# Ten of sixteen state-space scan units moved beside the q, k, v tiles, with decays loaded by DMA

## The chip, the cores and the metric

The program runs on one core of a Trainium2 chip. The metric is the device time of one execution in microseconds, as the median of several runs. The engines of the core each take their instructions in program order: TensorE (PE) multiplies matrices into PSUM banks, VectorE (DVE) and GpSimd (POOL) do element-wise work, ScalarE (ACT) evaluates functions such as Exp, and SyncE (SP) issues the DMAs. The engines meet at semaphores alone.

## The reference, cut to what matters

The program is a hybrid layer (a state-space branch, local attention with sinks, a mixture of experts) and then two further layers. The change lies in the first layer, in the state-space branch, beside local attention:

```
dt = softplus(dt_raw + dt_bias);  a_cum = cumsum(dt * a, within a chunk of 128)
xdt = xs * dt
decay[l,s] = exp(a_cum[l] - a_cum[s]) for l >= s, else 0
cb = cm @ bm^T                          # per group and chunk
y_diag = (cb * decay) @ xdt             # per head
states = bm^T @ (xdt * exp(a_cum[end] - a_cum))
carry  = carry * exp(a_cum[end]) + states
y_off  = (cm @ carry_before) * exp(a_cum)
y = y_diag + y_off + xs * d_skip;  out = rms_norm(y * silu(z))
```

There are 512 tokens, so four chunks of 128, and 32 heads in four groups of eight. Local attention has 16 query heads on 4 key-value heads, in four blocks of 128 tokens; each block sees itself and the one before.

## The kernel before

All of it is one list of stages; every stage is a function for each engine (PE, ACT, DVE, POOL, SP), and a stage's functions are simply written behind the last stage's on each engine. Semaphores (`Stage`, with a counter per engine) carry the dependences; a `Ring` of buffers makes a taker wait for the readers of the buffer's last use. `BR` and `XR` are rings over PSUM banks 0 to 3 and 4 to 7.

Weights are fp32 and come in pieces of 1024 columns per partition, 512 KB each. `load_pieces` (SP) loads a piece, `piece_hi` (ACT) rounds it to a high half, and `piece_lo` (DVE, in the z stage every second piece on POOL) subtracts to get the low half. A product then takes three PE passes for each of eight blocks of the depth (`dense`, L442 to L444; 24 matmuls of 512 columns).

The stages around the change:

- **dt** makes the step sizes, the running sums (`NAC` holds their negative, `EAC`, `DTE`, `CDC` their exponentials) and `DA`, the steps times a.
- **qkv** has 14 steps t: two k tiles, eight q tiles (each a dense product, squares, a block sum, a root by Ln and Exp, a norm product on DVE, a rotation on PE, a sine product and a sum on DVE, a cosine product on POOL), and four v tiles of 256 columns. The steps of a tile are spread: tile t's dense product, tile t-2's rotation and tile t-1's block sum stand together in step t.
- **mix** has 20 rounds. `MIX` is the order, written by hand, and every engine follows the same list. Round r holds `s0` of scan unit r (a unit is a group g and a chunk c, four chunks of a group in a row), `s1` of unit r-1, attention's steps `a2`, `a1`, `a0` of units r-2, r-1 and r, and from round 4 on two z tiles (24 matmuls of 256 columns each, tanh on ACT, silu product on DVE, product with y on POOL). `w` splits a piece of z's weights.

In `s0`, PE makes `cb`, and for eight heads the decay exponents: a mask product (L972) and, for each head, a product of `DA` against the triangle (L976). ACT takes Exp of them with the bias `NAC` (L1085), DVE copies cb and multiplies it in (the unit's *weights*, L1127). In `s1`, PE multiplies weights and `xdt` (L988), the carried state (L998) and the new state (L1006), and DVE adds the results up: L1134 always, L1140 and L1142 where c > 0, L1149 or L1153 and L1156 where c < 3. POOL prepares xdt (L1206), its decayed copy and the skip term.

- **out** follows: gates, projections, and the rest of the layer.

Of the kernel before, what the change touches and what calls it, by code (L numbers as in the profile page):

```python
# [7 lines left out]
F32 = mybir.dt.float32  # L8
# [144 lines left out]
def const_parts():  # L153
# [15 lines left out]
    parts["negbig"] = np.where(row > col, NEG, 0.0)  # L169
# [52 lines left out]
def build(nc, d, out):  # L222
    ctx = ExitStack()
    with ctx:
# [142 lines left out]
        WR1 = ring(LOADS, w_sems[0:4])  # L367
        WRZ = ring(LOADS[0:1], w_sems[0:1])
        WRZ.prior = [WR1.of(max(n for n in range(Z_FIRST) if n % 4 == 0))]
        WR3 = ring(LOADS, w_sems[0:4])  # L370
        WR3.prior = [WRZ.of(G_FIRST - 1)] + [WR1.of(max(n for n in range(Z_FIRST) if n % 4 == i)) for i in (1, 2, 3)]
        for r in (WRZ, WR3):
            r.restart()
# [3 lines left out]
        def raw(n):  # L377
            return WR1 if n < Z_FIRST else WRZ if n < G_FIRST else WR3

# [328 lines left out]
        NAC, EAC, DTE, CDC = tiles(4, 32), tiles(4, 32), tiles(4, 32), tiles(4, 32)  # L708
        work2 = top[0]
        dx, du, dw, dl, ea = alloc(128), alloc(128), alloc(128), alloc(128), alloc(32)  # L710
        DTT = alloc(512)

# [6 lines left out]
        def dt_pe(e):  # L719
# [28 lines left out]
            m.then_inc(*D.pe.up("total"))  # L748

        def dt_dve(e):  # L750
# [29 lines left out]
            e.tensor_tensor(DTE, v3(bb.ap[:, 0:128]), NAC, ALU.add).then_inc(*bb.free(D.dve, "dte"))  # L780

        def dt_act(e):
# [8 lines left out]
            e.activation(EAC, v3(ba.ap[:, 0:128]), ACT.Exp).then_inc(*ba.free(D.act))  # L791
            e.wait_ge(*D.dve.to("dte"))
# [5 lines left out]

        top[0] = work2
        HBX, HBQ = ring(bufs(4, 512)), ring(bufs(4, 512))  # L800
# [5 lines left out]
        def qkv_ahead(t):  # L806
            n = AT["k", t] if t < 2 else AT["q", t - 2] if t < 10 else AT["v", 1]
            return min(n + 2, Z_FIRST - 1)

        def qkv_sp(e):  # L810
            load_pieces(e, AT["k", 0], Z_FIRST)
# [7 lines left out]
        def qkv_pe(e):  # L819
            for t in range(14):  # L820
                if 1 < t < 10:
                    qkv_dense(e, t)
                elif t >= 10:
# [13 lines left out]
                    if t == 13:  # L837
                        WS1.of(ns[1]).frees.update(WS1.of(ns[0]).frees)
                if 0 <= t - 4 < 2:
                    b, x = XR.take("swap", t - 4), KT[:, 2 * (t - 4), :]  # L840
# [7 lines left out]
                if 0 <= t - 2 < 10:  # L848
                    b = XR.take("rot", t - 2)
# [3 lines left out]
                    e.matmul(b.ap[:, :], C["rot"], HBX.of(t - 2).ap, start=True, stop=True).then_inc(*K.pe.up("rot", t - 2))  # L853
                if 0 <= t - 1 < 10:
                    b = XR.take("blk", t - 1)
# [5 lines left out]
        def qkv_act(e):  # L861
            for t in range(14):
                piece_hi(e, qkv_ahead(t))
                if t < 10:
                    b, x, q = BR.of("qkv", t), HBX.take(t), HBQ.take(t)
                    for s, n in x.before + q.before:
                        e.wait_ge(s, n)
                    e.wait_ge(*K.pe.to("mm", t))
                    e.activation(x.ap, b.ap[:, :], ACT.Copy).then_inc(*K.act.up("cp", t))
# [2660 lines left out]
```

## Time and profile before

| | us |
|---|---|
| median of 3 runs | 2756.09 (2755.23 to 2756.17) |
| profiled execution | 2754.79 |
| its span | 2752.8 |
| PE busy in the span | 2578.9 |
| DVE / ACT / POOL busy | 1130.6 / 1037.7 / 843.0 |

Over the whole span PE is busy for 94% of the time, and 67% of the chain of work that ended last is PE's. In a table of stretches each engine has its busy microseconds with the number of its instructions, and then the clock that TensorE was granted (1.00 is 2.4 GHz, 0.50 is 1.2 GHz). In a timeline a row has start, duration, engine, line and operation, and in square brackets how long the engine had been idle before, and what ended that.

### The profile page before, as it was taken

What the parts mean: (1) busy time and instruction counts of PE and PEld (TensorE: products, weight loads), DVE (VectorE), ACT (ScalarE), POOL (GpSimd) and SP (SyncE); (2) the same over time, 40 slices, a digit from 0 to 9 for tenths busy, and PEclk for the clock granted to TensorE, in tenths of its full rate; (3) what the DMA queues carried; (4) which work ended last, traced back from release to release, by engine and by line L of the source; (5) the groups of instructions that cost most, each with busy time, mean ns of one, the idle gap of its engine ahead of it and who ended that gap; (6) DMA issues with size and microseconds to landing.
All of it is one profiled execution on the core that took longest, in us unless ns stands there. A gap on an engine that the chain in (4) does not pass through costs nothing.

```text
span 2752.8 us, 41999 instructions
## 1 busy us (share of the span) xinstructions
PE 2578.9 (94%) x16790; PEld 2120.6 (77%) x16790; DVE 1130.6 (41%) x2008; ACT 1037.7 (38%) x2142; POOL 843.0 (31%) x538
## 2 busy tenths in 40 slices
PE   7999899999978888888999989999999999999999
PEld 6877788888865555555888879999999887778877
DVE  7854666332232111111456653224247776412212
ACT  5444454432222211213455554322334555532231
POOL 1002565312321222200311105644641110465563
PEclk9999999999989999999999999999999999999999
DMA  4230111333349999998311112323322111233331
GB/s 147 82 83 23 32 32 39 108 92 92 104 170 390 426 426 426 427 423 337 93 47 55 47 39 73 97 79 91 100 78 77 47 52 42 61 89 95 100 99 62
DMA packets 311731, 370.43 MB, mean 135 GB/s; under 512 B 10208, under 2 KB 283744, under 8 KB 286960
## 3 DMA queue, kind: packets, MB, share of 16 engines
q1 hardware_dynamic: 310384, 363.52, 37.7%
q0 software_dynamic: 1152, 4.19, 0.4%
q8 instruction: 136, 2.23, 0.3%
q14 instruction: 59, 0.48, 0.1%
HBM read 363.49 MB, written 4.19 MB: 134 GB/s over the span
## 4 chain that ended last, share of the span: by engine, by line
PE 67%; DMA 12%; DVE 9%; ACT 5%; POOL 3%; issue 3%; SPq 0%; ACTq 0%; DVEq 0%; POOLq 0%
DMA early<-in_w_up_e 11%; PE bank L2406 5%; PE bank L1900 5%; PE bank L2407 5%; PE bank L2408 5%; PE bank L2913 4%; PE bank L2914 4%; PE bank L2915 4%; PE bank L442 4%; PE bank L444 4%; PE bank L443 4%; POOL split L2381 2%; DVE early L683 2%; PE bank L1060 1%; PE bank L1062 1%
## 5 line engine op out<-in xcount | busy, mean ns | idle before, releaser
L2381 POOL TENSOR_TENSOR split<-keep,split 128x1024 fp32r<-128x1024 f32 x143 | 352.3, 2468 | 452.7 <-ACT split L2355 452.7
L2406 PE MATMUL bank<-x_hi,split 128*128 128x264 f32 (+1 forms) x1280 | 396.9, 310 | 11.3 <-POOL split L2381 9.6
L2407 PE MATMUL bank<-x_lo,split 128*128 128x264 f32 (+1 forms) x1280 | 390.1, 305 | 0.0
L2408 PE MATMUL bank<-x_hi,split 128*128 128x264 f32 (+1 forms) x1280 | 389.8, 305 | 0.0
L2355 ACT ACTIVATE split<-keep 128x1024 fp32r<-128x1024 f32 x192 | 200.2, 1050 | 222.8 <-PE bank L2915 208.1
L1900 PE MATMUL bank<-early 128*64 128x256 f32 x2048 | 238.2, 386 | 38.0 <-DMA early<-in_w_up_e 32.6
L2406 PEld LDWEIGHTS bank<-x_hi,split 128*128 128x128 f32 x1280 | 240.9, 188 | 32.4 <-issue 19.2
L1900 PEld LDWEIGHTS bank<-early 128*64 128x64 f32 x2048 | 165.9, 139 | 121.1 <-issue 73.6
L2407 PEld LDWEIGHTS bank<-x_lo,split 128*128 128x128 f32 x1280 | 241.1, 188 | 9.9 <-issue 0.2
L2408 PEld LDWEIGHTS bank<-x_hi,split 128*128 128x128 f32 x1280 | 240.1, 188 | 10.2
L2951 DVE TENSOR_TENSOR mlp<-mlp,bank 128x264 f32<-128x264 f32 (+1 forms) x96 | 49.5, 515 | 326.6 <-ACT mlp L2930 326.6
L2913 PE MATMUL bank<-hidden0h,split 128*128 128x264 f32 x512 | 145.5, 284 | 1.2 <-issue 1.2
L2914 PE MATMUL bank<-hidden0l,split 128*128 128x264 f32 x512 | 145.1, 283 | 0.0
L2915 PE MATMUL bank<-hidden0h,split 128*128 128x264 f32 x512 | 145.0, 283 | 0.0
L414 ACT ACTIVATE w_split<-early 128x1024 fp32r<-128x1024 f32 (+1 forms) x101 | 105.6, 1046 | 100.7 <-PE bank L444 97.0
L2018 DVE TENSOR_TENSOR early<-early,bank 128x256 f32<-128x256 f32 x32 | 13.5, 421 | 314.4 <-PE bank L1941 189.4
L2961 DVE TENSOR_TENSOR mlp<-bank,roots 128x264 f32<-128x264 f32 (+1 forms) x96 | 46.8, 515 | 228.9 <-PE bank L2915 228.9
L1924 PE MATMUL bank<-early 128*64 128x512 f32 x512 | 116.9, 598 | 21.4 <-DVE early L2025 21.4
L428 DVE TENSOR_TENSOR w_split<-early,w_split 128x1024 fp32r<-128x1024 f32 (+1 forms) x70 | 89.9, 1284 | 95.3 <-ACT w_split L414 95.3
L442 PE MATMUL bank<-x_hi,w_split 128*128 128x512 f32 x304 | 123.8, 407 | 1.3 <-DVE w_split L428 0.7
L2930 ACT ACTIVATE mlp<-bank 128x264 f32<-128x264 f32 (+1 forms) x96 | 43.6, 454 | 202.4 <-PE bank L2408 202.4
L444 PE MATMUL bank<-x_hi,w_split 128*128 128x512 f32 x304 | 118.8, 391 | 0.0
(490 smaller groups left out, 6127.4 us busy)
## 6 DMA issues: line engine op xcount, KB each, us to landing
early<-in_w_gate_e SPq DMA_DIRECT2D x64, 1024.0 KB, 10.9
early<-in_w_up_e SPq DMA_DIRECT2D x64, 1024.0 KB, 11.8
early<-in_w_down_e SPq DMA_DIRECT2D x64, 1024.0 KB, 11.2
early<-in_w_in SPq DMA_DIRECT2D x68, 512.0 KB, 3.7
keep<-in_mlp_w_in SPq DMA_DIRECT2D x64, 512.0 KB, 3.9
keep<-in_mlp_w_out SPq DMA_DIRECT2D x64, 512.0 KB, 4.0
keep<-in_a_w_qkv SPq DMA_DIRECT2D x24, 512.0 KB, 3.6
early<-in_w_ssd_out SPq DMA_DIRECT2D x16, 512.0 KB, 3.9
```

The source lines that it names most:

```text
L442: e.matmul(o, hi[:, k, :], xh, start=first and k == 0, stop=False, skip_group_check=True)
L444: m = e.matmul(o, lo[:, k, :], xh, start=False, stop=last and k == 7, skip_group_check=True)
L1900: m = e.matmul(b.ap[cols(j, 64), o:o + 256], x.ap[:, k, cols(j, 64)], wtile(us[j], 8, 256)[:, k, :], start=k == 0, stop=k == 7, skip_group ...
L1924: m = e.matmul(b.ap[cols(j, 64), :], ht.ap[:, f * 128 + 64 * j:f * 128 + 64 * j + 64], wtile(us[j], 2, 1024)[:, f, cols(q, 512)], start=f ...
L2355: e.activation(hi, x, ACT.Copy).then_inc(*S.act.up("hi", n))
L2381: e.tensor_tensor(lo, x, whole(hi), ALU.subtract).then_inc(*u.free(sig_, "lo", n))
L2406: e.matmul(o, hi[:, k, :], xh, start=k == 0, stop=False, skip_group_check=True)
L2407: e.matmul(o, hi[:, k, :], xl, start=False, stop=False, skip_group_check=True)
L2408: m = e.matmul(o, lo[:, k, :], xh, start=False, stop=k == 7, skip_group_check=True)
L2913: e.matmul(o, hi[:, k, :], yh[:, k, n0 - at:n1 - at], start=k == 0, stop=False, skip_group_check=True)
L2914: e.matmul(o, hi[:, k, :], yl[:, k, n0 - at:n1 - at], start=False, stop=False, skip_group_check=True)
L2915: m = e.matmul(o, lo[:, k, :], yh[:, k, n0 - at:n1 - at], start=False, stop=k == 7, skip_group_check=True)
```

## The change

1. **Decays by DMA.** The dt stage also makes the running sums with heads on partitions (four small products, `acumT`), DVE copies them to `AROWS`, SP writes them to DRAM (`decay_rows`), and for each scan unit `decay_sp` loads the eight rows of the unit, broadcast to all partitions, 128 x 1024 values. ACT takes Relu of (own sum - row) with a bias for each head, eight times 128 columns, and one Exp of the negative over 1024 columns. The upper triangle is masked on DVE, when cb is read (`cb_dve`, in the place of the copy). The mask product and the eight products per unit are gone from PE.
2. **Ten units beside the tiles.** `cb_pe`, `decay_act`, `cb_dve` and `scan_pool` of unit t-4, and `scan_pe`, `weights_dve` and `scan_dve` of unit t-5 stand in step t of qkv, from t = 4. Rotation, swap and block sums use `BR` in place of `XR`; raw weight pieces have three buffers there in place of four; q and k are worked on in their final place.
3. **Mix has 19 rounds.** Round r holds s0 of unit r+10 and s1 of unit r+9, attention's a2, a1, b0 and a0 of units r-3, r-2, r-1 and r (b0 is the end of the softmax: denominator, reciprocal, probabilities), and z tiles from the first round on, two a round in 13 rounds, then one.
4. `weights_dve` of a unit stands in the round of its products, ahead of them, and no longer in the round before. The slot of the first of z's two split pieces is freed half-way in the last tile that reads it, and the first weights of out may be loaded as soon as their buffers are free.

```diff
+        K_FIRST = AT["k", 0]
+        WRQ = ring([LOADS[i] for i in (2, 3, 0)], [w_sems[i] for i in (2, 3, 0)])
...
+            br = XR.take("acumT")
...
+                m = e.matmul(br.ap[0:32, c * 128:c * 128 + 128], DA[:, c, :], C["upto"], start=True, stop=True, skip_group_check=True)
...
+        def decay_sp(e, i):
...
+            rows = arows[8 * g:8 * g + 8, 128 * c:128 * c + 128].unsqueeze(0).to_broadcast([128, 8, 128])
+            e.dma_start(h8(x.ap), rows).then_inc(*x.landing())
...
+        def decay_act(e, i):
...
+            for j in range(8):
+                h, y = g * 8 + j, x.ap[:, cols(j, 128)]
+                e.activation(y, y, ACT.Relu, bias=AC[:, c, h:h + 1], scale=-1.0).then_inc(*M.act.up())
+            e.wait_ge(*M.act.now())
+            e.activation(x.ap, x.ap, ACT.Exp, scale=-1.0).then_inc(*M.act.up("decay", i))
...
+            e.tensor_tensor(q.ap, b.ap[:, 0:128], C["upto"], ALU.mult).then_inc(*b.free(M.dve, "cb", i))
...
         def qkv_sp(e):
-            load_pieces(e, AT["k", 0], Z_FIRST)
+            done = K_FIRST
+            for t in range(14):
...
+                if t == 2:
+                    e.wait_ge(*D.dve.to("acumT"))
+                    e.dma_start(arows, AROWS[0:32, :]).then_inc(*d_arows.land(0))
+                    e.wait_ge(*d_arows.to(0))
+                if t + 1 >= S_FIRST:
+                    decay_sp(e, t + 1 - S_FIRST)
...
+                if t >= S_FIRST:
+                    cb_pe(e, t - S_FIRST)
+                if t > S_FIRST:
+                    scan_pe(e, t - 1 - S_FIRST)
...
                 piece_lo(e, qkv_ahead(t), False)
+                if t > S_FIRST:
+                    weights_dve(e, t - 1 - S_FIRST)
...
+        Z_ROUNDS = [[2 * r, 2 * r + 1] if r < 13 else [13 + r] for r in range(19)]
         MIX = []
...
+            MIX += [(f, r + S_BESIDE - lag) for f, lag in (("s0", 0), ("s1", 1)) if r + S_BESIDE - lag < 16]
+            MIX += [(f, r - lag) for f, lag in (("a2", 3), ("a1", 2), ("b0", 1), ("a0", 0)) if 0 <= r - lag < 16]
+            MIX += [("z", j) for j in Z_ROUNDS[r]]
...
-            e.wait_ge(*M.pe.to("pv", 15))
```

What VectorE has in its row for one tile of qkv before (L888 sine product, L891 sum, L897 norm product, L428 lo half of a weight piece):

```order
L428 TENSOR_TENSOR w_split_51<-early,w_split_51 128x1024 [waits wsplit_act]
L888 TENSOR_TENSOR early<-bank5,early 128x512 [waits qkv_pe]
L891 TENSOR_TENSOR early<-early 128x512 [waits qkv_pool,qkv_dve]
L897 SCALAR_TENSOR_TENSOR early<-early,lasting 128x512 [waits qkv_act]
```

And now, for a tile beside which a unit with c = 2 is scanned (L903 the unit's weights, L1058, L1061 and L1066 the tile's three, L897 the masked cb of the next unit, L911 to L933 the unit's results, then the next tile's lo half L429 and the next unit's weights):

```order
L903 TENSOR_TENSOR early<-early 128x1024 [waits mix_act,mix_dve]
L1058 TENSOR_TENSOR early<-bank0,early 128x512 [waits qkv_pe]
L1061 TENSOR_TENSOR early<-early 128x512 [waits qkv_pool,qkv_dve]
L1066 SCALAR_TENSOR_TENSOR early<-early,lasting 128x512 [waits qkv_act]
L897 TENSOR_TENSOR early<-bank7,lasting 128x128 [waits mix_dve,mix_pe]
L911 TENSOR_TENSOR early<-early,bank4 128x512 [waits mix_pool,mix_pe]
L917 TENSOR_TENSOR ints<-bank5,early 128x512 [waits mix_pe,mix_dve]
L919 TENSOR_TENSOR early<-early,ints 128x512 [waits mix_dve]
L930 TENSOR_TENSOR early<-early 128x512 [waits mix_dve,mix_pe]
L933 TENSOR_TENSOR early<-early,bank6 128x512 [waits mix_pe,mix_dve]
L429 TENSOR_TENSOR w_split_51<-early,w_split_51 128x1024 [waits wsplit_act]
L903 TENSOR_TENSOR early<-early 128x1024 [waits mix_act,mix_dve]
```

Seven instructions have come between one tile's norm product and the next tile's sine product. On PE, the same tile after its dense product, before (L853 rotation, L859 block sum):

```order
L853 MATMUL bank5<-early,lasting 128x512 [waits qkv_dve,qkv_act]
L859 MATMUL bank6<-early,lasting 128x512 [waits qkv_act]
```

And now (L849 cb of the next unit, L861 the unit's y products, L871 carried state, L879 new state, L1019 rotation, L1025 block sum):

```order
L849 MATMUL bank7<-early 128x128 [waits mix_dve]
L861 MATMUL bank4<-early 128x64 [waits mix_pool,mix_dve]
L861 MATMUL bank4<-early 128x64 x7
L871 MATMUL bank5<-early 128x512 [waits mix_dve]
L879 MATMUL bank6<-early 128x512 [waits mix_pool,mix_dve]
L1019 MATMUL bank1<-early,lasting 128x512 [waits qkv_dve,qkv_act]
L1025 MATMUL bank2<-early,lasting 128x512 [waits qkv_act,qkv_dve]
```

Rotation and block sum now stand behind products that wait for the unit's weights. In mix, VectorE at the turn of a round before (L1188 silu products of the two z tiles, L1124 and L1127 cb and weights of the unit that PE multiplies one round later, L1134 and L1149 results of the unit before):

```order
L1188 SCALAR_TENSOR_TENSOR early<-early,bank2 128x256 [waits z_act]
L1188 SCALAR_TENSOR_TENSOR early<-early,bank3 128x256 [waits z_act]
L1124 COPY early<-bank7 128x128 [waits mix_dve,mix_pe]
L1127 TENSOR_TENSOR early<-early 128x1024 [waits mix_act,mix_dve]
L1134 TENSOR_TENSOR early<-early,bank6 128x512 [waits mix_pool,mix_pe]
L1149 COPY early<-bank7 128x512 [waits mix_pe,mix_dve]
```

And now (L1273 silu products, L903 weights of the unit that PE multiplies in this round, L897 cb, L911 to L933 its results):

```order
L1273 SCALAR_TENSOR_TENSOR early<-early,bank2 128x256 [waits z_act]
L1273 SCALAR_TENSOR_TENSOR early<-early,bank3 128x256 [waits z_act]
L903 TENSOR_TENSOR early<-early 128x1024 [waits mix_act,mix_dve]
L897 TENSOR_TENSOR early<-bank5,lasting 128x128 [waits mix_dve,mix_pe]
L911 TENSOR_TENSOR early<-early,bank6 128x512 [waits mix_pool,mix_pe]
L917 TENSOR_TENSOR ints<-bank7,early 128x512 [waits mix_pe,mix_dve]
L919 TENSOR_TENSOR early<-early,ints 128x512 [waits mix_dve]
L930 TENSOR_TENSOR early<-early 128x512 [waits mix_dve,mix_pe]
L933 TENSOR_TENSOR early<-early,bank4 128x512 [waits mix_pe,mix_dve]
```

The weights are now those of the same round's y products, and stand behind the silu products of the round before.

## Rows read from the trace of the kernel before

**Rows 1.** Table of stretches: busy us (instructions) by engine, clock, DMA share, GB/s.

```profile
205.70:265.60 59.90, 59.90 (x278) 44.34 (x277) 24.87 (x34) 25.55 (x39) 14.05 (x12) 1.00 0.09 27
265.60:312.40 46.80, 38.17 (x244) 28.53 (x244) 26.81 (x56) 22.56 (x85) 20.25 (x16) 0.89 0.08 23
...
205.70:514.20 308.50, 296.07 (x2022) 244.30 (x2022) 177.66 (x295) 139.84 (x403) 145.78 (x108) 0.98 0.14 40
```

**Rows 2.** Chain that ended last, in order of time: start us, us, what.

```profile
220.59 1.06 PE bank L853 x2
...
352.79 0.86 PE bank L1006 x2
...
377.57 0.89 PE bank L976 x8
378.69 0.89 PE bank L976 x8
379.58 1.73 PE bank L988 x16
...
384.27 1.06 PE bank L1019 x8
```

**Rows 3.** Timeline of VectorE, then of ScalarE, in a q tile and a mix round.

```profile
228.88 0.69 DVE L888 TENSOR_TENSOR early<-bank,early 128x512 f32<-128x512 f32 x1 [2.53 <-PE bank L853]
...
232.33 1.22 DVE L428 TENSOR_TENSOR w_split<-early,w_split 128x1024 fp32r<-128x1024 f32 x1
236.08 0.69 DVE L888 TENSOR_TENSOR early<-bank,early 128x512 f32<-128x512 f32 x1 [2.53 <-PE bank L853]
...
230.46 0.63 ACT L880 ACTIVATE early<-early 128x512 f32<-128x512 f32 x1
231.00 1.04 ACT L414 ACTIVATE w_split<-early 128x1024 fp32r<-128x1024 f32 x1
...
423.64 2.16 ACT L1085 ACTIVATE early<-bank,early 128x128 f32<-128x128 f32 x8
```

**Rows 4.** DMA issues of the page: out<-in, queue, count, size, us to landing.

```profile
early<-in_w_in SPq DMA_DIRECT2D x68, 512.0 KB, 3.7
```

**Rows 5.** Groups of 262 to 516 us, then two lines: ns min/median/max.

```profile
L1134 DVE TENSOR_TENSOR early<-early,bank 128x512 f32<-128x512 f32 x16 | 10.8, 674 | 0.0
L1142 DVE TENSOR_TENSOR early<-early 128x512 f32<-128x512 f32 x12 | 12.5, 1041 | 0.4
L1153 DVE TENSOR_TENSOR early<-early 128x512 f32<-128x512 f32 x8 | 8.0, 998 | 0.0
...
L1127 DVE TENSOR_TENSOR early<-early x16: 1224/1459/3357, 270.6 to 469.1; 128x1024 f32<-128x1024 f32 x16
...
L1206 POOL TENSOR_TENSOR early<-early x16: 1037/1756/2039, 263.1 to 471.3; 128x512 f32<-128x512 f32 x16
```

**Rows 6.** Timeline of ScalarE, VectorE and GpSimd at the last z tiles.

```profile
488.10 0.39 ACT L1115 ACTIVATE early<-bank 128x256 f32<-128x256 f32 x1 [2.29 <-PE bank L1062]
490.98 0.39 ACT L1115 ACTIVATE early<-bank 128x256 f32<-128x256 f32 x1 [2.49 <-PE bank L1062]
...
491.39 0.42 DVE L1188 SCALAR_TENSOR_TENSOR early<-early,bank 128x256 f32<-128x256 f32 x1 [2.46 <-ACT early L1115]
...
492.59 2.40 POOL L428 TENSOR_TENSOR w_split<-early,w_split 128x1024 fp32r<-128x1024 f32 x1
```

**Rows 7.** PE's timeline after three gaps, and stretches after the first and third.

```profile
288.20 2.07 PE L998 MATMUL bank<-early 128*128 128x512 f32 x2 [4.03 <-DVE early L1124]
...
309.59 1.13 PE L998 MATMUL bank<-early 128*128 128x512 f32 x2 [2.16 <-DVE early L1124]
...
501.18 0.35 PE L1060 MATMUL bank<-w_split,x_hi 128*128 128x256 f32 x1 [3.34 <-DVE w_split L428]
...
290.00:294.00 4.00, 4.00 (x11) 1.35 (x9) 3.11 (x5) 0.39 (x1) 1.94 (x2) 0.50 0.27 95
...
502.30:505.60 3.30, 3.30 (x18) 3.30 (x17) 0.00 (x0) 0.00 (x0) 0.00 (x0) 0.51 1.05 297
```

More of the change, by code:

```diff
@@ L707, in build @@
         top[0] = work
-        NAC, EAC, DTE, CDC = tiles(4, 32), tiles(4, 32), tiles(4, 32), tiles(4, 32)
+        NAC, EAC, DTE, CDC, AC = (tiles(4, 32) for _ in range(5))
         work2 = top[0]
@@ L796, in build @@
         program.append((dt_pe, dt_act, dt_dve, None, dt_sp))
+        M = Stage("mix")
+        ZS = Stage("z")
         top[0] = work2
-        HBX, HBQ = ring(bufs(4, 512)), ring(bufs(4, 512))
+        HBQ_ = bufs(3, 512)
+        HBQ = ring(HBQ_)
+        CBR, XD = ring(bufs(1, 128)), ring(bufs(1, 512))
+        AROWS = alloc(512)
+        XE = ring([AROWS])
+        STATE = ring(bufs(2, 512))
+        ex_sems = [sig(f"decay{i}_landed") for i in range(2)]
+        EX = ring([alloc(1024), LOADS[1]], ex_sems)
@@ new lines, in build, with h8, cols @@
+        EX.prior = [None, WR1.of(max(n for n in range(K_FIRST) if n % 4 == 1))]
+        EX.restart()
+        TMP = ring([IT[:, 0:512].bitcast(F32)])
+        assert top[0] <= NA - 16
+        SSD_UNITS = [(g, c) for g in range(4) for c in range(4)]
+        S_FIRST, S_BESIDE = 4, 10
+        def h8(a):
+            return a.rearrange("p (j n) -> p j n", j=8)
+        def cols(i, n):
+            return slice(i * n, i * n + n)
+        def decay_sp(e, i):
+            g, c = SSD_UNITS[i]
+            x = EX.take(i)
+            for s, n in x.before:
+                e.wait_ge(s, n)
+            rows = arows[8 * g:8 * g + 8, 128 * c:128 * c + 128].unsqueeze(0).to_broadcast([128, 8, 128])
+            e.dma_start(h8(x.ap), rows).then_inc(*x.landing())
@@ L923, in build @@
-        ZR = ring(bufs(2, 256))
-        MASK = halves("mask", top[0], 2, 128)
-        top[0] += 256
-        IDENTR, NEGR = MASK[:, 0, :], MASK[:, 1, :]
+            for t in range(2, 14):
+                if t < 12:
+                    x = qkv_out(t - 2)
+                    e.wait_ge(*K.dve.to("sin", t - 2))
+                    e.tensor_tensor(x, x, COS, ALU.mult).then_inc(*K.pool.up("cos", t - 2))
+                if t == S_FIRST:
+                    e.wait_ge(*X.act.to("turned", 15))
+                    e.wait_ge(*D.act.to("done"))
+                    e.wait_ge(*d_arows.to(0))
+                if t >= S_FIRST:
+                    scan_pool(e, t - S_FIRST)
@@ L1075, in mix_act @@
                 if what == "s0":
[L1076 to L1086 removed]
+                    decay_act(e, i)
                 if what == "a0":
```

335 lines of the change are left out of this document (168 added, 167 removed).

## The prediction

> **What bounds the kernel now.** I read the table of stretches first [rows 1], because the change touches only what lies between the fifth of the q, k, v tiles (205.7 us) and the last z tile (514.2 us). In these 308.5 us TensorE is busy for 296.1 us. The first stretch (tiles 4 to 13) has no gap at all; the second (four mix rounds without z tiles) has 8.6 us of gaps; and 3.3 us before 501.2 are one more [rows 7], which leaves 0.5 us of gaps for all the rounds with two z tiles. So PE bounds this part, and the change can win only what it takes off PE, plus those gaps. VectorE is busy for 177.7 us of the 308.5, ScalarE 139.8, GpSimd 145.8: no engine but PE is near its limit by its sum. What decides is therefore the order in which each engine meets its work, not the sums.
>
> **What it removes.** Each scan unit loses two mask products and eight products against the triangle on PE. The chain shows one half of a unit at 0.89 us for its eight records, and 1.12 us from one half to the next (378.69 after 377.57, with the mask product between) [rows 2]. So 16 units x 2 x 1.12 = 35.8 us leave PE. With all gaps closed as well (12.4 us) the stretch could shrink by 48.2 us at most. The four new products for the running sums (four of 128 columns, under 1 us) stand in the dt stage, ahead of the stretch; I take them at nothing, since they are ready before PE's next product has its squares, and at 1 us if not.
>
> **What it adds.** On ScalarE eight Relu of 128 columns, priced like the eight Exp they replace (2.16 us together [rows 3]), and one Exp over 1024 columns. No row has that; a copy of 1024 columns takes 1.04 [rows 3], so I take 1.05; the eight Exp of 128 before, at 2.16, bound it above. The DMA per unit is 512 KB in pieces of 512 bytes, like one weight piece: 3.7 us to landing [rows 4]. A unit's load leaves when products of the unit two before are done, about two tiles ahead of its use, so even 15 us would be hidden. On SP weight loads stand behind it, with a tile or more in hand.
>
> **What it moves: the tiles.** In the new order VectorE does in tile t: lo half of a weight piece, weights of unit t-5, sine product, sum, norm product, mask product of unit t-4, results of unit t-5. PE does in tile t: dense, products of unit t-5, rotation t-2, block sum t-1. The weights of the *next* unit thus stand behind the norm product, which waits for ScalarE's root, which waits for the block sum, which PE does after the products of *this* unit. That is a closed cycle. Count from the start S of the sine product:
> - VectorE: to the end of the norm product 3.5 us (228.88 to 232.4, where the lo half follows it [rows 3]); mask product 0.3 (128 columns); results of the unit. These are 1.35 us where c is 0 (two operations that read PSUM, 0.67 each), 4.1 where c is 1 or 2 (three that read PSUM, and two between SBUF tiles of 1.04 and 1.0), 2.4 where c is 3 [rows 5]; then lo 1.22 [rows 3] and weights 1.25 (the lower end of rows 5: GpSimd is mostly through by then).
> - ScalarE: root ready at S+2.2 (230.46 + 0.63 [rows 3]), Relu and Exp 3.3, then hi 0.95 more: the lo half can't start before S+6.45.
> - So the weights are done at S+9.0 (c 0 or 3, by ScalarE) or S+10.4 (c 1 or 2, by VectorE). Then PE: 1.75 us for eight y products, about 0.9 each for carried state and new state [rows 2], 1.05 to the sine product.
>
> The dense tile takes 7.2 - 1.9 = 5.3 us (distance of sine products without swap, less rotation and block sum [rows 3]), so PE is through with it at S+6.4 and waits. S of tile 4 is at 213.5 (205.7 + 5.3 + 0.2 + 1.0 swap + 1.05, rounded up). The next steps: 13.6 (with the second swap), 13.5, 14.9, 14.0, 12.6, 11.2 (no piece to split), 14.1; that is 307.4. Then the weights of unit 7 after 10.1, its products 2.65, and tiles 12 and 13 with unit 8 about 5.9: tiles end at **326.1** instead of 265.6, +60.5 us, with ten units masked and nine multiplied. PE idles in gaps of 2.6, 2.6, 4.0, 4.0, 2.6, 2.7, 5.6 and 7.1 us there.
>
> **What it moves: the mix.** Now a round starts on PE with the y products of a unit, whose weights VectorE makes after the *second* z product of the round before. PE ends its z tile, tanh starts 0.4 us later, the silu product ends at +1.2 (490.98, 491.39 [rows 6]), weights 1.25 more: 2.5 us of gap, less 0.2 for the mask matrix. After every second round a piece's hi and lo halves stand ahead of the weights: 2.3 us more. A z tile is 2.88 us [rows 6], attention 1.0 for each of its three PE steps [rows 2] (half for the first block row), and the exponentials end before the second z tile does, as before, so they cost nothing. From weights to weights: 14.3, 12.1, 14.0, 12.3, 16.0, 13.7 = 82.4. The first round is 2 us late, because its second z piece is loaded behind the decays of unit 10 on SP. 326.1 + 1.7 (first weights) + 2 + 82.4 = 412.2; + 11.1 to the end of that round: 423.3. Rounds 7 to 12 have no scan: 8.8 each on PE; in every other one the lo half on GpSimd (2.40 us [rows 6], behind its z product) holds the z tiles up by 1.4: 57.0. Rounds 13 to 18 with one z tile: 5.9, then 7.1 and 9.2 (scores wait for a bank behind the exponentials; in round 15 for the piece), then 4.9, 4.9, 3.9: 35.9. The end: **516.2**. The 3.3 us wait before 501.2 [rows 7] is gone within that.
>
> So order and durations alone give 516.2 against 514.2, **+2.0 us**: all that PE is rid of comes back as PE waiting for VectorE.
>
> **Two things on top.** After gaps PE's clock falls. After 4.03 us without work (288.20) a pair of records of 512 columns took 2.07 us in place of 1.06 [rows 2], and PE was still at 0.50 (1.2 of 2.4 GHz) until 294; after 2.16 us (309.59) the pair took 1.13, so the clock held; after 3.34 us (501.18) it ran at 0.51 for 3.3 us [rows 7]. Of the gaps counted above seven are over 3.2 us and seven between 2.0 and 2.7; I take half of these too. A spell of 3.3 us at half speed loses 1.6 us of PE work, and that work lies on the cycle: 10.5 x 1.6 = 17 us. The bounds are 0 and 14 x 3 (spells of 6 us, like the one from 288 to 294) = 42. Second, VectorE's operations between SBUF tiles stretch when GpSimd works: the 1024-column one from 1.22 to 3.36, and the two of 512 columns take 1.04 and 1.0 on average where those that read PSUM take 0.67 [rows 5]. These means are in the sum already; GpSimd's three products now stand beside the sum and the norm product of each tile. I add 3 us (bounds -5, all unhindered, to +15).
>
> The Trainium skill (SBUF — State Buffer, "two separate sides") says that a VectorE operation with two SBUF inputs and a GpSimd operation exclude each other for a whole instruction. The stretched rows agree. If VectorE lost every race to GpSimd's three products of 1.05 us (the lower end in rows 5), the rule would make it 3 us in each of some 13 cycles, 41 us in place of my 3; the means in the rows are well under that.
>
> **Sum.** +2 + 17 + 3 = +22 us. The profiled execution took 2754.8 (span 2752.8 and 2.0 around it), 1.3 below the median; against the median 2756.1: **2778**. Nothing after 514 us changes its order, and out's first weights are loaded earlier than they are needed in both kernels, so the shift is carried to the end.
>
> **Rivals.**
> - *Clock holds, GpSimd stays out of the way.* The cycles close as counted, yet gaps cause no half-speed spells, and the 2.04 us of work between SBUF tiles in each unit with c 1 or 2 shrinks to the 1.35 of operations that read PSUM (eight units, 5.5 us). 516.2 - 5.5 = 510.7, 3.5 below; with 0.1 us off each of the 25 or so waits that I rounded up it is 6 below: some 2750. For it: gaps of 2.0 to 2.6 are the commoner ones. Against it: both gaps over 3.2 us in the rows were followed by half speed. It decides if fewer than two spells occur. Faster: 0.12.
> - *The cycle is not there.* If weights were always ready, PE would bound as before: 2756 - 48 = 2708. Each wait above is one engine's fixed order, so this needs durations 3 us shorter per cycle. 0.02, within the faster case.
> - *A tie.* A few spells only, 2757 to 2761: 0.16.
> - *Worse.* Most gaps bring the long spell, and GpSimd's products win the port: 42 + 15 on top of 2, less what overlaps, some +48: 2804. 0.22.
> - *Forecast*, 2762 to 2792: 0.48.
>
> An edit of 0.2% (5.5 us) is about what a measurement can tell from no change. Faster 0.14, same 0.16, slower 0.70. The range 2752 to 2806 leaves out the big gain and the far tails.
>
> **What would show it.** Right: PE's first y product of each unit in tiles 5 to 12 preceded by 2.5 to 7 us of idle time released by VectorE's weights; sine products 12 to 16 us apart instead of 7.2; tiles ending near 326 to 340 us; the mix stage some 190 to 200 us long instead of 248.6; PE's clock at half speed in many of the spells after these gaps; no wait for the decay loads. Wrong: sine products 11 us apart (PE bound), y products that follow the dense tile at once, or ScalarE waiting for decays to land.

## The result, and the profile after

| | us |
|---|---|
| median before, on the same chip | 2756.13 (2755.23 to 2757.68) |
| median after | **2809.78** (2808.63 to 2812.76) |
| ratio after / before | 1.0196, 95% interval 1.0178 to 1.0213 |
| profiled execution after, its span | 2808.63, 2806.8 |

The change makes the kernel slower by 53.7 us. The forecast was slower by 22 (2778), and its range ended at 2806: the direction was right, the size was not.

The busy time of the engines in the page of the changed kernel:

```profile
PE 2585.2 (92%) x16510; PEld 2114.5 (75%) x16510; DVE 1145.8 (41%) x2009; ACT 1055.8 (38%) x2157; POOL 826.5 (29%) x538
```

PE has some 36 us less to do and is busy for 6 us *longer* than before (2585.2 against 2578.9). The table of stretches of the changed kernel says why; its columns are those of [rows 1], and the four stretches are the tiles, the passage to the mix, the rounds with scan products, and the rest up to z's end:

```profile
205.70:355.50 149.80, 118.32 (x472) 85.45 (x470) 70.10 (x87) 58.12 (x128) 43.28 (x35) 0.78 0.17 44
355.50:367.00 11.50, 0.06 (x1) 0.00 (x0) 2.88 (x3) 5.18 (x11) 4.39 (x4) 0.58 0.31 91
367.00:480.00 113.00, 95.25 (x544) 75.00 (x545) 53.86 (x107) 44.12 (x129) 43.05 (x37) 0.79 0.22 57
480.00:574.00 94.00, 90.36 (x717) 77.14 (x717) 44.74 (x102) 51.43 (x152) 42.00 (x33) 1.00 0.21 59
...
205.70:574.30 368.60, 304.29 (x1734) 237.89 (x1733) 171.58 (x296) 158.85 (x418) 132.72 (x108) 0.83 0.20 53
```

Two things are to be seen against [rows 1]. The stretch is 368.6 us long where it was 308.5, with 64.3 us of PE's idle time where there were 12.4. And the granted clock is 0.78 and 0.79 in two long stretches, 0.83 over the whole, where it was 0.98. So PE both waits and runs slowly between its waits.

PE's timeline at the y products of units 1 and 2 (tiles), 9 (the first round), 10, 14 and 15. A row's own time is that of 16 short records, the bracket is the idle time ahead of it:

```profile
240.63 3.00 PE L861 MATMUL bank<-early 128*128 128x64 f32 x16 [2.58 <-DVE early L903]
...
259.51 3.65 PE L861 MATMUL bank<-early 128*128 128x64 f32 x16 [4.37 <-DVE early L903]
...
367.25 3.65 PE L861 MATMUL bank<-early 128*128 128x64 f32 x16 [11.69 <-DVE early L903]
...
383.17 2.25 PE L861 MATMUL bank<-early 128*128 128x64 f32 x16 [1.89 <-DVE early L903]
...
449.40 3.52 PE L861 MATMUL bank<-early 128*128 128x64 f32 x16 [1.95 <-DVE early L903]
...
468.67 3.65 PE L861 MATMUL bank<-early 128*128 128x64 f32 x16 [4.06 <-DVE early L903]
```

Every one is preceded by idle time that the unit's weights (L903) end: the waits are where the forecast put them. Most are also as long as it put them: in the tiles 2.6, 4.4, 4.4 and 2.6 us ahead of units 1 to 4, where it had 2.6, 4.0, 4.0 and 2.6, and about 2 and 4 in turn in the mix. Ahead of units 5 to 7 they are 3.8 to 3.9 (forecast 2.7, 5.6 and 7.1 ahead of units 5, 6 and 7), ahead of unit 8 there is none, and ahead of unit 9 the wait is three times the forecast's. What the forecast made too small is the second column. The 16 records take 1.9 to 2.0 us at full clock (rows further down); here they take from 2.25 to 3.65, the latter being half speed throughout, and this after gaps of 1.9 us as well as after those of 4.

VectorE and ScalarE between two sine products of the changed kernel, in the cycle that the forecast described:

```profile
254.41 0.68 DVE L917 TENSOR_TENSOR ints<-bank,early 128x512 f32<-128x512 f32 x1
255.12 0.69 DVE L919 TENSOR_TENSOR early<-early,ints 128x512 f32<-128x512 f32 x1
255.73 0.68 DVE L930 TENSOR_TENSOR early<-early 128x512 f32<-128x512 f32 x1
...
258.19 1.22 DVE L903 TENSOR_TENSOR early<-early 128x1024 f32<-128x1024 f32 x1
266.92 0.69 DVE L1058 TENSOR_TENSOR early<-bank,early 128x512 f32<-128x512 f32 x1 [7.51 <-PE bank L1019]
269.09 1.45 DVE L1061 TENSOR_TENSOR early<-early 128x512 f32<-128x512 f32 x1 [1.48 <-POOL early L1082]
270.46 1.53 DVE L1066 SCALAR_TENSOR_TENSOR early<-early,lasting 128x512 f32<-128x512 f32 x1
```

The weights are ready at 259.41, and the next sine product (L1058) starts 7.5 us later. At full clock PE needs 4.6 us for what lies between (y products at 258.17, sine product at 262.73 in the kernel with six needless products, below).

### The profile page after: what moved, and what is told of

Same layout as the page of the kernel before. It is cut to its first block, busy times and chain, and to the rows that moved or that the text cites. A ratio compares the mean times of both kernels' runs of the same rounds, so it can differ in the third digit from the quotient of the medians.

```text
span 2806.8 us, 41459 instructions
## 1 busy us (share of the span) xinstructions
PE 2585.2 (92%) x16510; PEld 2114.5 (75%) x16510; DVE 1145.8 (41%) x2009; ACT 1055.8 (38%) x2157; POOL 826.5 (29%) x538
## 4 chain that ended last, share of the span: by engine, by line
PE 64%; DMA 12%; DVE 9%; issue 6%; ACT 5%; POOL 5%; SPq 0%; ACTq 0%; DVEq 0%; POOLq 0%
DMA early<-in_w_up_e 11%; PE bank L2478 5%; PE bank L2480 5%; PE bank L2479 5%; PE bank L1972 5%; PE bank L2985 4%; PE bank L2986 4%; PE bank L2987 4%; PE bank L443 3%; PE bank L444 3%; PE bank L445 3%; POOL split L2453 2%; DVE early L684 2%; PE bank L861 1%; PE bank L1186 1%
## 5 line engine op out<-in xcount | busy, mean ns | idle before, releaser
L2090 DVE TENSOR_TENSOR early<-early,bank 128x256 f32<-128x256 f32 x32 | 13.5, 421 | 314.9 <-PE bank L2013 198.1
L429 DVE TENSOR_TENSOR w_split<-early,w_split 128x1024 fp32r<-128x1024 f32 (+1 forms) x70 | 87.4, 1248 | 103.6 <-ACT w_split L415 103.6
## 6 DMA issues: line engine op xcount, KB each, us to landing
early<-in_w_gate_e SPq DMA_DIRECT2D x64, 1024.0 KB, 11.2
```

## The experiments

The theory from the trace (**the clock**): the order itself costs little, as forecast, and the rest is PE at half speed after each wait. Its rivals: the order costs more than was counted, in the tiles' cycle, in the mix rounds or at the passage between them.

### Needless products in the waits

```diff
             for s, n in b.before:
                 e.wait_ge(s, n)
+            for _ in range(3 if i < S_BESIDE - 1 else 2):
+                e.matmul(b.ap[:, :], C["ones"], R[:, 0, 16:T2], start=True, stop=True, skip_group_check=True)
             e.wait_ge(*M.dve.to("weights", i))
```

> The changed kernel, with idle gaps of TensorE filled: ahead of each wait for a unit's weights PE makes three needless products (two in the mix rounds) of 512 columns, 0.86 us each, into the bank that the y products then overwrite. Nothing else changes, and the weights come no earlier. Theory A (the half-speed clock after each gap is what I under-sized): the products after each gap run at full speed, the stretch from weights to sine product falls from about 8 to about 4.5 us in seven tiles (24 us) and the rounds with a scan lose about 3 us each (15 to 18 us): 2765 to 2780 us. Theory B (the length of VectorE's and GpSimd's chain is the cost, the clock only goes with it): within 5 us of 2810, as the chain is no shorter; if the filler delays the weights' users, slower.

Measured: 2787.55 us (2783.37 to 2790.09), ratio 1.012 (1.010 to 1.014), so 22 us less by adding work to PE. That is short of what the clock theory wanted. The trace of this kernel says why; two y products and the stretch of the tiles:

```profile
251.98 2.46 PE L863 MATMUL bank<-early 128*128 128x64 f32 x16 [1.76 <-DVE early L905]
...
284.16 2.00 PE L863 MATMUL bank<-early 128*128 128x64 f32 x16 [0.41 <-DVE early L905]
...
205.70:355.50 149.80, 129.94 (x556) 86.50 (x554) 76.58 (x94) 64.19 (x138) 49.74 (x40) 0.92 0.21 53
```

Three products (2.6 us) don't fill a wait of over 4 us. The 1.76 us that stay idle are followed by slow records (2.46), the 0.41 by full speed (2.00), and the clock comes back to 0.92 only.

### Twice as many

The same with `range(6 if i < S_BESIDE - 1 else 4)`.

> The changed kernel with six needless products of 512 columns (four in the mix rounds) ahead of each unit's y products, where three (two) gave 2787.6 us and left 2.3 us of idle time before each. Six take 3.5 us at full clock, so they should close the gaps but for the one of 11.7 us. Nothing of VectorE's or ScalarE's work is changed. Theory A (half speed follows any idle time here, and the order alone costs 2 to 10 us over the kernel before): with no gap left the granted clock is over 0.97 in 205 to 355 us and the time falls to 2760 to 2780, though the needless products themselves delay the y products where weights come early. Rival B (most of the loss is the order itself, the clock was worth just the 22 us that three products gave back): 2785 to 2800.

Measured: 2795.37 us (2791.10 to 2797.42), ratio 1.0138 (1.0121 to 1.0155): by its number a hit for the rival. But the tiles of this kernel read:

```profile
205.70:355.50 149.80, 141.06 (x588) 90.46 (x586) 71.42 (x87) 59.98 (x129) 48.13 (x38) 1.00 0.19 50
...
253.02 5.32 PE L859 MATMUL bank<-lasting 128*128 128x512 f32 x12
258.17 1.89 PE L863 MATMUL bank<-early 128*128 128x64 f32 x16
```

The clock is 1.00, as theory A wanted. Six products take 5.32 us, though, and not the 3.5 that I had expected of them. This unit's weights ended at 257.47 and its y products began at 258.17, 0.7 us late; for other units it is up to 4.2 us. Over the nine units beside the tiles these delays sum to some 18 us, each on the cycle. So this run could not tell the theories apart, and it called for one that fills the waits to their length.

### Filled to the length of each wait, and only the long ones filled

```diff
-            for _ in range(3 if i < S_BESIDE - 1 else 2):
+            for _ in range([3,3,5,5,3,2,4,4,1,13,2,4,2,4,3,4][i]):
```

and, for the second kernel, `[0,0,5,5,0,0,4,4,1,13,0,4,0,4,0,4]`.

> The changed kernel with as many needless products of 512 columns (0.86 us each) before each unit's y products as fit into its wait and no more: 3, 3, 5, 5, 3, 2, 4, 4, 1 for units 0 to 8, 13 for unit 9, then 2, 4, 2, 4, 3, 4. The waits are those of the kernel with six and four of them, from the start of the first needless product to the end of the unit's weights (2.6, 2.6, 4.5, 4.5, 3.1, 2.3, 3.7, 3.7, 1.0, 12.0, 2.0, 3.9, 2.2, 3.9, 2.7, 4.2 us), so y products start when the weights are there and PE is idle for less than 0.9 us ahead of each. Theory A (all that the needless products did in that kernel was to keep the clock, and to be late by 0.7 to 4.2 us per unit, 17.7 us in the tiles and 3.1 in the mix): that kernel's 2795.4 less 20.8 and less the 2 us of half speed after unit 9's wait, 2773; from the changed kernel's side, 2809.8 less some 42 of clock, 2768. So 2764 to 2776, the last z product at 530 to 536 us, the granted clock 0.98 or more from 205 us on. Rival B (part of the loss is in the order itself, in waits that shift as soon as PE is faster): 2780 to 2790.

> The same, but only the waits over 3.5 us are filled (units 2, 3, 6, 7, 9, 11, 13, 15; unit 8 keeps its one); the seven waits of 1.9 to 3.1 us (units 0, 1, 4, 5, 10, 12, 14) stay idle. Theory A (in this order a gap of about 2 us brings half speed by itself, and the forecast that only half of them do was wrong): each costs what the section between y products and sine product is longer in the changed kernel than in the one with six needless products, 3.4, 3.4, 1.8 and some 2.7 in the tiles and about 1.9 in each of three mix rounds, 17 us: 2780 to 2792, with the first y products of these units at 2.3 to 3.7 us for 16 records in place of 1.9. Rival B (the short gaps fell to half speed only because long ones stood around them): within 4 us of the kernel in which all are filled.

Measured: **2766.40** us (2763.33 to 2768.51), ratio 1.0043 (1.0026 to 1.0060), with all waits filled, and 2788.98 (2783.04 to 2793.26), ratio 1.0117 (1.0097 to 1.0138), with only the long ones filled. Both are what theory A wanted. The first kernel: its stretch up to z's end, the y products of unit 2, and a last z product:

```profile
205.70:533.00 327.30, 313.94 (x1870) 231.48 (x1870) 179.15 (x298) 160.39 (x422) 136.71 (x109) 1.00 0.23 63
...
252.95 2.00 PE L863 MATMUL bank<-early 128*128 128x64 f32 x16
...
530.78 0.28 PE L1190 MATMUL bank<-w_split,x_hi 128*128 128x256 f32 x1
```

The order is the same, there is some needless work more on PE, and the time is 43.4 us less (42 by the two ratios): that is the price of the clock in this change. The durations on the other engines are the same but for some of VectorE's beside GpSimd: four units' weights took 1.36 to 2.06 us there, and 1.22 in the changed kernel. What is left over the kernel before is about 12 us (2766.4 against the 2754.6 measured beside it).

In the second kernel the gaps of about 2 us are back:

```profile
240.27 3.39 PE L863 MATMUL bank<-early 128*128 128x64 f32 x16 [2.56 <-DVE early L905]
...
302.49 3.65 PE L863 MATMUL bank<-early 128*128 128x64 f32 x16 [3.52 <-DVE early L905]
...
368.07 1.97 PE L863 MATMUL bank<-early 128*128 128x64 f32 x16 [2.30 <-DVE early L905]
369.88 1.65 PE L873 MATMUL bank<-early 128*128 128x512 f32 x2
...
368.00:374.00 6.00, 5.93 (x28) 3.50 (x28) 3.31 (x5) 2.31 (x6) 4.88 (x4) 0.72 0.34 72
```

Seven gaps left open, the longest of them 3.52 us, cost 22.6 us by the medians (3.2 each) and 18 by the traces at z's end (549.1 against 531.1, 2.6 each; expected 17), with no other wait unfilled. So the gaps of 2 to 3.5 us bring half speed by themselves, not because longer ones stood around them. The last three rows show that the y products alone don't tell it: after 2.30 us their 16 records still ran at full clock, but the carried state right behind them took 1.65 us instead of 1.08, and the clock over the 6 us is 0.72. The same holds behind the open gap of 2.57 us at 224.59 (1.97 us for the 16 records, clock 0.71 from there to 230).

### Unit 9's weights in the last tile step

```diff
                 if t > S_FIRST:
                     scan_dve(e, t - 1 - S_FIRST)
+            weights_dve(e, S_BESIDE - 1)
...
-                    weights_dve(e, i - 1)
+                    if i > S_BESIDE:
+                        weights_dve(e, i - 1)
                     cb_dve(e, i)
```

> The changed kernel, but the weights of unit 9 are made at the end of the q, k, v steps on VectorE, ahead of the low half of z's second piece and no longer behind it. PE stands for 11.7 us before the y products of unit 9 (355.6 to 367.2). If that wait is the low half's, which waits for the load of z's second piece, which waits for the low half of the first on GpSimd: y products of unit 9 start near 357.5, and 6 to 10 us are saved unless the z tiles wait for the same piece behind them: 2800 to 2806. If the decays of unit 9 or their load are late instead: no change, 2810.

Measured: 2803.61 us (2801.32 to 2808.04), ratio 1.0172 (1.0152 to 1.0193): 6 us less, as expected. That is little more than the spread of the executions, but in the traces, too, the y products of unit 15 start 6.6 us earlier (462.08 against 468.67). What the edit gets around is the wait of 11.69 us ahead of 367.25. These are the rows of the changed kernel on GpSimd, SyncE, ScalarE and VectorE in that wait:

```profile
357.69 2.34 POOL L429 TENSOR_TENSOR w_split<-early,w_split 128x1024 fp32r<-128x1024 f32 x1
360.06 0.37 SPq L392 DMA_DIRECT2D early<-in_w_in  x1
363.70 1.06 ACT L415 ACTIVATE w_split<-early 128x1024 fp32r<-128x1024 f32 x1 [6.30 <-DMA early<-in_w_in]
...
364.79 1.23 DVE L429 TENSOR_TENSOR w_split<-early,w_split 128x1024 fp32r<-128x1024 f32 x1 [8.62 <-ACT w_split L415]
365.93 1.22 DVE L903 TENSOR_TENSOR early<-early 128x1024 f32<-128x1024 f32 x1
```

GpSimd splits z's *first* piece, behind its scan products; only then is the buffer free and the second piece loaded; ScalarE rounds it, VectorE splits it, and the weights stand behind that. With the weights ahead of it, unit 9's y products start at 358.19, and the wait for the second piece shows up later, in front of a z product. Rows of this kernel:

```profile
358.19 3.65 PE L861 MATMUL bank<-early 128*128 128x64 f32 x16 [2.35 <-DVE early L903]
368.34 0.55 PE L1187 MATMUL bank<-w_split,x_hi 128*128 128x256 f32 x1 [2.71 <-DVE w_split L429]
```

### The tiles' cycle opened

```diff
-                if t > S_FIRST:
-                    scan_pe(e, t - 1 - S_FIRST)
                 if 0 <= t - 4 < 2:
...
                     e.matmul(b.ap[:, :], C["blk"], HBQ.of(t - 1).ap, start=True, stop=True).then_inc(*K.pe.up("blk", t - 1))
+                if t > S_FIRST:
+                    scan_pe(e, t - 1 - S_FIRST)
```

> The changed kernel, but in the q, k, v steps PE makes a unit's products behind the rotation and the block sum of that step in place of ahead of them. Theory of the cycle (weights, products, rotation, sine, norm product, results, low half, weights): it is cut, so sine products come 11 to 13 us apart in place of 15 to 18, the tiles end 20 to 40 us earlier: 2770 to 2790. Rival (VectorE's sum of work in a tile beside GpSimd bounds): no gain over 5 us. If the clock is still half after the gaps that are left, the gain is at the lower end.

Measured: 2751.81 us (2749.92 to 2757.86), ratio 0.9987 (0.9975 to 1.0000): 58 us less than the change as made, by moving one line past two. The sine product no longer waits for the scan products, and so the next weights don't wait for the last ones. The stretch of nine steps of the tiles, and the sine product with the weights ahead of it:

```profile
199.40:282.90 83.50, 82.22 (x391) 60.24 (x390) 57.90 (x72) 52.71 (x110) 34.65 (x29) 1.00 0.29 78
...
223.00 1.22 DVE L903 TENSOR_TENSOR early<-early 128x1024 f32<-128x1024 f32 x1
224.14 0.68 DVE L1058 TENSOR_TENSOR early<-bank,early 128x512 f32<-128x512 f32 x1
...
226.88 1.53 DVE L1066 SCALAR_TENSOR_TENSOR early<-early,lasting 128x512 f32<-128x512 f32 x1
```

PE is busy for 82.2 of 83.5 us at full clock, and sine products are 7.5 to 10.9 us apart where a unit is scanned beside them (15.0 to 18.3 in the changed kernel). I had expected 2770 to 2790: I had priced the waits and not the clock that comes back with them.

### Weights one round ahead in the mix

```diff
-                    weights_dve(e, i - 1)
+                    if i == S_BESIDE:
+                        weights_dve(e, i - 1)
                     cb_dve(e, i)
...
-                    if i == 15:
-                        weights_dve(e, i)
                     scan_dve(e, i)
...
                     e.tensor_scalar(q.ap[:, 4:8], q.ap[:, 0:4], -1.0, None, ALU.mult).then_inc(*M.dve.up("max", i))
+                    if i + S_BESIDE < 16:
+                        weights_dve(e, i + S_BESIDE)
```

> The changed kernel, but in the mix rounds VectorE makes a unit's weights behind attention's maximum of the round before, ahead of the z products, as the kernel before did, and not at the start of the unit's own round. If the weights' place is what makes PE wait 1.9 to 4.1 us at the start of six rounds (with half speed behind each), these gaps vanish: 17 us of gaps and about 15 us of slow products, so 2780 to 2790. Rival (the decays on ScalarE or VectorE's sum bound the rounds): under 8 us of gain.

Measured: 2776.20 us (2774.58 to 2778.25), ratio 1.0074 (1.0054 to 1.0094): 34 us less, and again more than I had expected (2780 to 2790). The y products of a later unit and the stretch of the mix, where the clock was 0.79:

```profile
402.87 1.97 PE L861 MATMUL bank<-early 128*128 128x64 f32 x16 [0.38 <-DVE early L903]
...
367.00:480.00 113.00, 109.73 (x808) 92.57 (x808) 79.19 (x144) 62.94 (x190) 60.30 (x50) 0.96 0.26 71
```

### All three, and then z's first piece earlier

The three edits together; and with them

```diff
+                if t == 12:
+                    piece_lo(e, Z_FIRST, True)
                 if t >= S_FIRST:
                     scan_pool(e, t - S_FIRST)
...
+                if t == 13:
+                    load_pieces(e, Z_FIRST + 1, Z_FIRST + 2)
```

> Three edits of the changed kernel at once, each of which alone gave: scan products behind rotation and block sum in the q, k, v tiles (-58 us), weights of a mix round made one round ahead, behind attention's maxima (-34 us), weights of unit 9 at the end of the tiles (-6 us). Theory A (each edit cures a separate place: the tiles' cycle, the mix rounds' wait, the first round's wait, and with the gaps gone the clock stays up): they add, 2810 - 58 - 34 - 6 = 2712, range 2702 to 2722; TensorE's granted clock 0.95 or more in 367 to 480 us. Rival B (the share of the clock was counted in two of the edits at once, and TensorE's own gaps elsewhere take its place): 2730 to 2745. If TensorE had the 35.8 us of decay products taken off it and no new wait put in, before's 2756 would become 2720; with its old gaps closed too, 2708.

> The same three edits, and the first z piece is split on GpSimd and the second loaded beside the last tiles, so that the wait of some 10 us between the tiles and the mix, where GpSimd's half of the first piece stands ahead of the load of the second, should go. Theory A (that chain, GpSimd's half, load, ScalarE's half, VectorE's half, is what the first round waits for once unit 9's weights are early): 3 to 8 us less than with the three edits alone, 2705 to 2715, and the idle time of TensorE between 270 and 320 us falls by that much. Rival B (something else, ScalarE's or VectorE's queue at the end of the tiles, is late there too): no difference, within 2 us.

Measured: **2713.89** us (2713.27 to 2718.75), ratio **0.9854** (0.9837 to 0.9870), and 2716.93 (2711.51 to 2719.67), ratio 0.9862 (0.9846 to 0.9879). The three edits add (2810 - 98 = 2712); at z's end the traces have 6.6, 55.2 and 33.0 us for the edits alone and 95.9 for all three. The result beats the kernel before by 43 us, and its last z product ends at 478.9 instead of 514.2, 35.3 us earlier: nearly all of the 35.8 us that the change takes off PE. The stretch, to be read against [rows 1] and the 368.6 us above:

```profile
205.70:478.60 272.90, 258.71 (x1736) 209.77 (x1736) 178.94 (x296) 157.97 (x418) 133.89 (x108) 0.99 0.27 73
```

258.7 us of work at full clock is what PE has to do here. In the changed kernel the same products kept it busy for 304.3: the difference, 45.6, is half speed, and agrees with the 43.4 us of the filled kernel.

The fourth edit brings nothing: its median is 3 us higher, within the spread of both kernels' executions, so its rival was right. With the weights early, the last wait of the tiles is another. ScalarE, VectorE and PE, in the kernel with three edits:

```profile
297.51 2.45 ACT L888 ACTIVATE early<-early 128x128 f32<-128x128 f32 x8 [4.22 <-DMA early<-decay_rows]
...
301.14 1.80 DVE L903 TENSOR_TENSOR early<-early 128x1024 f32<-128x1024 f32 x1 [0.86 <-ACT early L890]
...
303.04 3.54 PE L861 MATMUL bank<-early 128*128 128x64 f32 x16 [3.36 <-DVE early L903]
```

Unit 9's exponentials wait for its decays to land. Their load leaves when unit 7's products have freed the buffer (291.66), and lands 5.9 us later; in quick tiles that is no longer early enough. With the fourth edit the same load leaves still later, and ScalarE stands idle for 9.18 us ahead of 300.59. GpSimd, VectorE, PE and SyncE in that kernel:

```profile
285.55 2.83 POOL L429 TENSOR_TENSOR w_split<-early,w_split 128x1024 fp32r<-128x1024 f32 x1
286.06 2.87 DVE L930 TENSOR_TENSOR early<-early 128x512 f32<-128x512 f32 x1
...
290.89 3.57 PE L861 MATMUL bank<-early 128*128 128x64 f32 x16 [3.01 <-DVE early L903]
...
294.49 0.36 SPq L842 DMA_DIRECT2D early<-decay_rows  x1
```

GpSimd's half of z's first piece now runs beside VectorE's results of unit 6, and one of them takes 2.87 us instead of 0.68. So the weights of unit 7 come 2.2 us later (counted from the tile's sine product), PE waits 3.01 us instead of 0.82, and its y products take 3.57 us instead of 1.97. They free the buffer at 294.46, and unit 9's load leaves right then. The piece's added transfer stands behind this load on SP (294.90), not ahead of it. What the edit took away in one place it put back in another.

## Why the prediction was right or wrong

Forecast, the kernel with filled waits (the order at full clock) and the changed kernel, in us from one mark to the next:

| from, to | forecast | filled | changed |
|---|---|---|---|
| sine product of tile 4, at | 213.5 | 214.3 | 214.2 |
| to that of tile 11 | 93.9 | 98.3 | 120.5 |
| to y products of unit 9 | 22.4 | 30.3 | 32.6 |
| to y products of unit 15 | 82.4 | 85.9 | 101.4 |
| to the end of z | 104.0 | 102.3 | 106.1 |
| end of z | 516.2 | 531.1 | 574.8 |

- **What PE is rid of: right.** 35.8 us were counted, 35.3 appear as soon as no wait eats them (three edits).
- **The closed cycle: right.** Opening it in one place gave 58 us. Its seven steps, forecast 13.6, 13.5, 14.9, 14.0, 12.6, 11.2, 14.1, were 14.1, 13.7, 15.5, 14.7, 13.3, 12.3, 14.7 at full clock.
- **The clock: the term that failed.** "Seven are over 3.2 us and seven between 2.0 and 2.7; I take half of these too. A spell of 3.3 us at half speed loses 1.6 us of PE work": 10.5 x 1.6 = 17. Measured: 43.4 by time, 43.7 by the table (22.2 + 2.3 + 15.5 + 3.8, less 0.1). Both factors were low. Of the 16 units' y products, 15 came after a gap of 1.9 us or more, and half speed followed each. And the slow work was 2.9 us per gap (43.4 / 15), not 1.6. Over the 8 us from the start of the y products the granted clock was 0.79 behind two of the 15 gaps, which is 1.7 us of work lost, close to the forecast's 1.6; behind the other 13 it was 0.50 to 0.64, 2.9 to 4.0 us lost. From y products to sine product the seven tiles took 5.5 to 8.9 us instead of 3.8 to 5.0, so the spell covered most of the section between the two, all but a little of it in two tiles, and this section lies on the cycle. [Rows 7] gave the two spells of the kernel before, 3.3 and some 6 us, and I priced all of them by the shorter one; the bound for the longer one, 42, was the right number. A gap of 2.16 us after which the clock held [rows 7] was one case, and I gave it a weight of one half; behind none of the 63 gaps of 1.76 us or more ahead of y products in all these kernels did the clock hold.
- **The first z piece: the second miss, 8 us.** "The first round is 2 us late, because its second z piece is loaded behind the decays of unit 10 on SP." With 1.7 for the weights that made 3.7 us of wait; it was 11.69. The named queue was the wrong one: z starts with an odd piece, so its first piece is split on GpSimd and its second on VectorE, and load, ScalarE, VectorE and weights follow one after the other. Not all of it was on the path: early weights gave 6 us.
- **GpSimd and VectorE: right in the sum, by two errors.** In each tile the sum (L1061) and the norm product took 1.45 and 1.53 us; before, at 231.06 and 231.67, they took 0.69 and 0.74. So the norm product ended at S+5.07 and not at S+3.5. But the scan results between SBUF tiles, counted at 1.04 and 1.0, took 0.69 and 0.68 in the tiles. Three us were added for this. The filled kernel is 4.4 us over the forecast in the tiles and 3.5 in the mix, with whatever else the order was miscounted by in it; I haven't taken these two apart. The Trainium skill (SBUF — State Buffer, "two separate sides") has the loser of such a race blocked for the whole instruction of the other. The 1.45 and 1.53 agree with that; the 41 us that this would have cost if it hit the path in every cycle didn't come, since each tile lost 1.5 us to it and not 3, since in about half of the cycles (units 0, 1, 4 and in part 5) ScalarE is through as late as VectorE, and since the weights (L903) ran at 1.22 us in all 16 units of the changed kernel.
- **The mix and the end: right at full clock.** 85.9 against 82.4 for the rounds with scan, 102.3 against 104.0 for the rest.
- **"The shift is carried to the end": 6.6 us too much.** z ends 60.6 us later than before (574.8 against 514.2), the span is 54.0 longer. Four of the 6.6 us come back in one place, just after the experts. The kernel before has there, in PE's timeline and in its stretch:

```profile
1307.26 0.51 PE L2233 MATMUL bank<-place,yk_lo 128*128 128x512 f32 x1 [2.15 <-issue]
...
1304.00:1312.00 8.00, 5.67 (x17) 4.23 (x18) 2.59 (x4) 3.44 (x8) 0.00 (x0) 0.79 0.35 100
```

and the changed kernel, in the stretch that answers to it:

```profile
1362.00:1370.00 8.00, 7.37 (x34) 5.97 (x33) 2.59 (x4) 4.07 (x9) 0.00 (x0) 1.00 0.25 69
```

  The pause of 2.15 us and the slow spell behind it are missing. From the first of these products to the first of the next stage it is 31.5 us instead of 35.5, 31.4 to 31.5 in seven of the experiments, and 33.1 in the two with six needless products and with only the long waits filled. Why the pause is there before, and whether it is in every execution of it, stays open. So does the whole 6.6: from z's end to the end of the span the kernel before takes 2238.6 us and the changed one 2232.0, but the experiments, whose instructions there are the changed kernel's, take 2231.5 to 2242.4. With one profiled execution of each, it isn't shown that the change gives this time back.
- **"No wait for the decay loads": wrong, and without cost there.** In the changed kernel ScalarE waits for them ahead of units 8 and 9, which nobody waits for; with three edits it becomes the last wait of the tiles. The mistake was "about two tiles ahead of its use": a load leaves when the unit two before has been multiplied, for unit 9 at 346.95, and by then ScalarE had been idle for 7.6 us.

The sum then reads: order +2 forecast, +16.9 measured (531.1 against 514.2: the piece 8, the tiles' cycle 4.4, the mix 3.5, the rest -1.0 on top of 2); clock +17 forecast, +43.7 measured; given back -6.6; 54.0 us of span in all. The rival "worse" had the mechanism (most gaps bring the long spell) and came nearest, at 2804; its 15 us for GpSimd were not what was measured, and the first z piece and the longer cycle took their place by chance.

## What to carry to other kernels

Before moving work beside a pipeline, follow each engine's queue once round: when a step's input stands behind work that waits for the step before, the moved work sets the period, and one line in another place opens the ring. Price a recurring wait on TensorE as the wait plus slow work behind it, up to the whole section behind it at half speed (here 2.9 us more on a section of 4.6), and if a gap comes back in every iteration, count all of them, not the share that one row suggests. To learn what the clock alone costs, fill each wait to its own length with needless products: a fixed number left part of the loss (three) or added delays of its own (six).

## What the runs showed of the hardware

In the ten kernels that have the change, 96 of the 160 y products came after a gap. The granted clock over the 6 us from the start of each, beside the time of its 16 records (1.97 to 2.04 us at full clock behind a gap):

| gap, us | how many | granted clock over the 6 us |
|---|---|---|
| 0.18 to 1.28 | 33 | 1.00 behind 32; 0.72 behind one of the three of 1.28 us |
| 1.76 to 2.63 | 27 | 0.50 to 0.72 behind all |
| 2.79 to 11.71 | 36 | 0.50 to 0.72 behind all |

Behind six of these 63 longer gaps (1.95, 2.30, 2.30, 2.48, 2.57 and 3.36 us) the 16 records themselves still took 1.97 to 2.09 us, and half speed began with the end of them or right behind. So a quick first instruction behind a gap is no sign that the clock held: the granted clock of the stretch has to be read. The kernel before has a gap of 2.16 us behind which the clock was 1.00 for 8 us [rows 7], ahead of a carried state, and in the changed kernels one gap of 1.28 us brought half speed and two did not. The length of the last gap alone doesn't decide; what else does was not measured.
